# Summing a modulation part's two chunks side by side in a two-block transformer kernel on one Trainium2 core

## What is computed

```
c_act = silu(c)
mod = c_act @ w_mod[l] + b_mod[l]
sh_m, sc_m, g_m, sh_f, sc_f, g_f = split(mod, 6)
h = rms_norm(x, norm_mix_g[l]) * (1.0 + sc_m) + sh_m
x = x + g_m * mixer(h, ...)
h = rms_norm(x, norm_ffn_g[l]) * (1.0 + sc_f) + sh_f
x = x + g_f * moe_ffn(h, ...)
```

## Time and profile before

| | |
|---|---|
| median of 3 runs | 2131.26 us (2130.9 to 2132.2) |
| profiled execution, its own time | 2132.88 us |
| its span, first to last instruction | 2131.1 us |
| PE busy | 2043.1 us (96%) |
| DVE busy | 958.8 us (45%) |
| ACT busy | 404.0 us (19%) |
| mean granted TensorE clock | 0.985 |

### The profile page before, as it was taken

The page is one execution under the profiler, slowest core; times in us unless marked ns, Lnnn a source line. Parts: engine busy times, 40 slices in busy tenths (PEclk is TensorE's granted clock), DMA queues, the critical chain, the costliest instruction groups (busy, mean ns, idle before and its releaser), DMA issues. The chain is left out here.

```text
span 2131.1 us, 29148 instructions
## 1 busy us (share of the span) xinstructions
PE 2043.1 (96%) x10772; PEld 1105.8 (52%) x10772; DVE 958.8 (45%) x1926; ACT 404.0 (19%) x803; POOL 59.6 (3%) x143
## 2 busy tenths in 40 slices
PE   5999999899999999989999989999999997999998
PEld 2845544544545455466544454544545453475475
DVE  3797534433334333359865253333333333253252
ACT  2133211011111111123231111111111111232131
POOL 1000003000000000000000030000000000110000
PEclk9999999999999999999999989999999999999999
DMA  9664548699999999767454448999999997432621
GB/s 348 190 218 173 198 153 339 259 421 405 392 406 401 405 409 391 316 225 229 158 213 182 180 177 334 402 406 399 405 404 400 404 404 249 151 93 68 219 75 45
DMA packets 148386, 599.06 MB, mean 281 GB/s; under 512 B 13052, under 2 KB 17760, under 8 KB 96864
## 3 DMA queue, kind: packets, MB, share of 16 engines
q1 hardware_dynamic: 146912, 595.10, 72.6%
q0 software_dynamic: 1408, 3.10, 0.7%
HBM read 597.11 MB, written 1.05 MB: 281 GB/s over the span
## 5 line engine op out<-in xcount | busy, mean ns | idle before, releaser
L1232 PE MATMUL banks<-weight_ring,h_t 128*64 128x512 f32 x2112 | 464.6, 592 | 3.3 <-DVE h_t L1987 3.3
L867 PE MATMUL banks<-weight_ring,h_t 128*128 128x512 f32 x768 | 335.1, 593 | 2.4 <-issue 1.5
L1232 PEld LDWEIGHTS banks<-weight_ring,h_t 128*64 128x64 f32 x2112 | 152.9, 137 | 302.8 <-issue 301.0
L867 PEld LDWEIGHTS banks<-weight_ring,h_t 128*128 128x128 f32 x768 | 145.1, 190 | 181.2 <-issue 178.7
L1220 PEld LDWEIGHTS banks<-z,sp_ 128*128 128x128 bf16 x3168 | 179.7, 99 | 58.5 <-issue 51.9
L2012 DVE SCALAR_TENSOR_TENSOR o_parts<-banks,slot_weight,o_parts 128x512 fp32r<-128x512 f32 x132 | 99.2, 751 | 245.9 <-ACT o_parts L1523 245.9
L1992 DVE TENSOR_TENSOR z<-banks,z 128x256 f32<-128x256 f32 x66 | 28.1, 425 | 386.4 <-ACT z L1510 386.4
L1220 PE MATMUL banks<-z,sp_ 128*128 128x128 bf16 x3168 | 191.2, 221 | 4.9 <-DVEq L1977 4.9
L1270 PE MATMUL banks<-o_parts,slot_of 128*128 128x512 f32 x528 | 140.7, 408 | 6.0 <-issue 5.6
L1523 ACT ACTIVATE o_parts<-banks,slot_weight 128x512 fp32r<-128x512 f32 x132 | 90.7, 687 | 277.3 <-PE banks L1257 277.3
L2249 PE MATMUL banks<-weight_ring,h_t 128*128 128x512 f32 (+2 forms) x384 | 135.9, 514 | 0.7 <-DMA weight_ring<-in_w_in 0.4
(11 more groups left out here) (479 smaller groups left out, 1896.2 us busy)
## 6 DMA issues: line engine op xcount, KB each, us to landing
weight_ring<-in_w SPq DMA_DIRECT2D x264, 1024.0 KB, 10.0
weight_ring<-in_w_in SPq DMA_DIRECT2D x36, 2048.0 KB, 10.3
slots<-in_w SPq DMA_DIRECT2D x68, 1024.0 KB, 9.2
weight_ring<-in_w_mod SPq DMA_DIRECT2D x24, 2048.0 KB, 11.6
qk<-in_w SPq DMA_DIRECT2D x32, 1024.0 KB, 8.5
z<-in_w SPq DMA_DIRECT2D x32, 1024.0 KB, 10.5
weight_ring<-in_w_out SPq DMA_DIRECT2D x8, 2048.0 KB, 7.8
weight_ring<-in_w_in SPq DMA_DIRECT2D x10, 1024.0 KB, 12.3
```

Source lines behind the costliest of these rows:

```text
L867: mm = nc.tensor.matmul(bank[:, 0:cols], stationary[:, k, t * P:(t + 1) * P], w[:, k, 0:cols], start=(k == 0), stop=(k == KT - 1))
L1232: mm = nc.tensor.matmul(h_bank[own, :], x_blk[:, i, k, own], w13(2 * i + b)[:, :, k, :], start=(k == 0), stop=(k == KT - 1), skip_group_ch ...
```

## The change

Five things are edited.

1. The sum step of the two chunks of a column part becomes one step, `("cols", c)`: chunk `c` is summed with a 64-column stationary into partitions 0 to 63 of a bank, chunk `c + 1` into partitions 64 to 127 of the same bank. VectorE picks once for both, with `ident_half` (the sum of the identity's halves, made once at the start), and `mod_columns` no longer adds halves. Row parts keep their sums.
2. The places: `("sum", 6)` stood after the value projections and is gone; `("cols", 6)` stands ahead of the turns of `a`, `("cols", 8)` behind them; VectorE's pick of chunk 6 moves from behind the rotation to behind `a_ready`, ahead of `mod_on_dve(9)`.
3. `("cols", 12)` stands where the sum of 13 stood, and nothing where the sum of 12 did; `("cols", 14)` replaces two sums.
4. At the start the turns of the tokens stand ahead of the first part; ScalarE takes the norm ahead of its copies; the partial rows go through three buffers instead of two; four banks are skipped.
5. `c` is loaded first, SyncE no longer waits for GpSimd, and TensorE raises the eight bank semaphores in its place.

```diff
 MOD_STEPS = {
-    "start": [("part", 0), ("part", 1), ("sum", 0), ("part", 2), ("sum", 1), ("part", 3), ("sum", 2), ("sum", 3)],
-    "ka": [("sum", 4), ("sum", 5)], "va": [("sum", 6)], "aT": [("sum", 7), ("sum", 8), ("sum", 9)],
+    "first": [("part", 0), ("part", 1), ("cols", 0), ("part", 2), ("pad", 0), ("pad", 1), ("pad", 2), ("pad", 3),
+              ("part", 3), ("cols", 2)],
+    "ka": [("sum", 4), ("sum", 5)], "a": [("cols", 6)], "aT": [("cols", 8)],
     "merged": [("sum", 10), ("sum", 11)],
 }
-MOD_NEXT = {"mT": [("part", 12)], "wo": [("part", 13), ("sum", 12)], "turned": [("part", 14), ("sum", 13)],
-            "rt": [("part", 15), ("sum", 14), ("sum", 15)]}
+MOD_NEXT = {"mT": [("part", 12)], "wo": [("part", 13)], "turned": [("part", 14), ("cols", 12)],
+            "rt": [("part", 15), ("cols", 14)]}
...
-                            pe.wait_ge(B[l]["mod_part", c].free, B[l]["mod_part", c].consumed_at(l))
-                            mm = nc.tensor.matmul(bank[:], K.part_share[:].to_broadcast([P, P]), mod_part[c], start=True, stop=True)
+                            for half in range(2):
+                                own = slice(64 * half, 64 * half + 64)
+                                if c in DVE_CHUNKS:
+                                    pe.wait_ge(dve_parts.sem, dve_parts.at(l, c + half - DVE_CHUNKS[0] + 1))
+                                    share = K.ones[:, 0:64]
+                                else:
+                                    pe.wait_ge(B[l]["mod_part", c + half].free, B[l]["mod_part", c + half].consumed_at(l))
+                                    share = K.part_share[:].to_broadcast([P, 64])
+                                mm = nc.tensor.matmul(bank[own, :], share, mod_part[c + half], start=True, stop=True,
+                                                      skip_group_check=True)
...
-                mod("start")
-
                 norm_turn(0, l)
+                mod("first")
...
-                mod("va")
...
                         branch(2, h, t)
+                mod("a")
                 pe.wait_ge(a_ready.sem, a_ready.at(l))
...
-                mod((6,))
                 conv_taps(28, TAPS)
...
                 dve.drain().then_inc(a_ready.sem, 1)
+                mod(6)
                 mod_on_dve(9)
...
-                mod((7, 8, 9))
+                mod(8)
                 mod_columns(1)
```

More of the change, by code:

```diff
@@ L313, in vector_part @@
         dve.wait_ge(from_pool, masks_ready)
+        nc.vector.tensor_tensor(K.ident_half[:], K.ident[:, 0:64], K.ident[:, 64:P], ALU.add)
+        dve.drain()
         dve.wait_ge(from_act, tables_ready)
@@ L348 @@
 DVE_CHUNKS = range(4, 12)
-MOD_NEXT = {"mT": [("part", 12)], "wo": [("part", 13), ("sum", 12)], "turned": [("part", 14), ("sum", 13)],
-            "rt": [("part", 15), ("sum", 14), ("sum", 15)]}
+MOD_NEXT = {"mT": [("part", 12)], "wo": [("part", 13)], "turned": [("part", 14), ("cols", 12)],
+            "rt": [("part", 15), ("cols", 14)]}
 def mod_steps(place, layer):
-    if place == "start" and layer > 0:
+    if place == "first" and layer > 0:
         return []
@@ L363, in mod_groups @@
 def mod_groups(place, layer):
-    return [("mod_" + what, c) for what, c in mod_steps(place, layer)]
+    return ["-pad" if what == "pad" else ("mod_" + what, c) for what, c in mod_steps(place, layer)]
 def groups_1(layer):
@@ L373, in _groups_1 @@
     return (
-        mod_groups("start", layer) + [("xT", 0, g) for g in range(4)]
+        [("xT", 0, g) for g in range(4)] + mod_groups("first", layer)
         + [(n, i) for n in ("ug", "ua") for i in range(2)] + ["vec"] + [(n, i) for n in ("qc", "kc") for i in range(2)]
@@ L378, in _groups_1 @@
         + [("suf", r, par) for r in range(3) for par in range(2)]
-        + [(n, t) for n in ("vc", "va") for t in range(T)] + mod_groups("va", layer)
+        + [(n, t) for n in ("vc", "va") for t in range(T)]
         + [("oc", i) for i in range(2)]
@@ L383, in _groups_1 @@
         + [x for h in range(2) for t in range(T) for x in branch_groups(2, h, t)]
-        + [("aT1", i) for i in range(2)] + ["aT0"] + mod_groups("aT", layer)
+        + mod_groups("a", layer) + [("aT1", i) for i in range(2)] + ["aT0"] + mod_groups("aT", layer)
         + [("oa", t) for t in range(T)] + [("gt", 0, 0, 0)] + [("oaT", i) for i in range(2)] + [("gt", 0, 0, 1)]
@@ L899, in norm_turn @@
                             mm.then_inc(B[l]["xT", i, g].full, 1)
+            for b in range(BANKS):
+                pe.sem_inc(free[b].sem, 1)
             const_tensor(pe)
@@ L1587, in mod @@
                         else:
-                            v.tensor_tensor(pick, bank[:].rearrange("p (q k) -> p q k", k=KT),
-                                            broadcast(K.ident[:, 64 * half:64 * half + 64], 2, KT), ALU.mult)\
-                                .then_inc(B[l]["mod_sum", c].free, 1)
+                            bank = full_of(("mod_cols", c), l)
+                            v.tensor_tensor(pick, bank[:].rearrange("p (q k) -> p q k", k=KT), broadcast(K.ident_half[:], 2, KT),
+                                            ALU.mult).then_inc(B[l]["mod_cols", c].free, 1)
                             dve.drain()
-                            v.tensor_reduce(col4[:, MOD_COL_PARTS.index(part), half, :], pick.rearrange("p q k -> p k q"),
-                                            AX.X, ALU.add)
+                            v.tensor_reduce(col4[:, MOD_COL_PARTS.index(part), :], pick.rearrange("p q k -> p k q"), AX.X, ALU.add)
                             dve.drain()
@@ L1653, in _ @@
                 if l == 0:
-                    mod(range(MOD_FIRST))
+                    mod(0, 2)
                 if l == 0:
```

37 lines of the change are left out of this document (16 added, 21 removed).

## The result

| | before | changed |
|---|---|---|
| median of 6 runs | 2132.06 us (2130.90 to 2144.93) | 2150.7 us (2147.46 to 2154.06) |
| ratio, 95% interval | | 1.0085 (1.0065 to 1.0105) |
| profiled execution, its own time | 2132.88 us | 2147.46 us |
| its span | 2131.1 us | 2145.7 us |

The changed kernel is slower, as forecast, and by more: 2150.7 where 2144.0 was predicted, 0.7 us beyond the end of the stated range (2150). On the profiled executions the difference is 14.6 us, where the sum said 12.8.

The account below looks back on a forecast made before the run. TensorE, busy 96% of the span, was taken as nearly the critical path. +12.7 + 4.4 − 1.8 − 1.6 − 0.9 = +12.8 us gave 2145.7 us profiled, 2144.0 us against the median; range 2138.5 to 2150.

Parts of the forecast that it names:

- the term of the savings: Sum 6's removal −1.8 us, the start −1.6 and `cols 14` at the router −0.9.
- the way from one profiled execution to a median: Profiled execution forecast at 2145.7 us; its 1.6 us above the median taken off, giving 2144.0.
- The stall: Attention, both layers: TensorE waits for pick and chunk 9's rows; loop 10.25 us for 3.89, +12.7 us in all.
- The off-path rival: Attention: VectorE's loop costs nothing, only savings stay, including −1.7 us at `a`; 2125.3 us, chance 0.03.
- The clock: Behind both attention waits the granted clock falls from 2.4 to 1.2 GHz: 2.2 us per layer, +4.4 us.
- The rivals without the fall: Attention: the wait comes but the clock stays high behind it, −4.4 us, 2139.6 us; chance 0.10.
- with a long one: Attention: small matmuls hold the clock low for longer, +9.2 us over both layers, 2153 us; chance 0.06.
- Sum 6: Chunk 6's sum leaves its old place in two layers, where TensorE had no wait: −1.8 us.
- `cols 14`: Around the router, first layer: one joined step for the two sums of chunks 14 and 15, −0.9 us.
- the start: Kernel start: one pick instead of two, one add less, earlier weights; half clock stays: −1.6 us, ends 0 and −4.
- Halves side by side: Every pair of 64-column halves: the two overlap on TensorE and take 0.86 us a pair.
- Rival "a pass late": At three places on the path a pair's second half begins 0.43 us late: +1.3 us, 2145.3 us; chance 0.15.

Follow-up runs that it names:

- the filled run: Changed kernel with six extra 64-column matmuls per layer in TensorE's wait ahead of the second half of `cols 8`: 2142.11 us, ratio 1.0054.
- The order alone: Kernel before with full sums and its old start and router, only chunk 6's sum and pick moved to the changed places: 2153.88 us, ratio 1.0102.
- a fourth buffer: Changed kernel with a fourth buffer for partial rows, so VectorE makes chunk 9's rows ahead of the pick of chunks 6 and 7: 2133.23 us, ratio 1.0003.
- an earlier sum: Changed kernel with `cols 6` on TensorE between the first branch's two column halves, ahead of VectorE's pick: 2133.93 us, ratio 1.0004.
- the start alone: Kernel before with only the change's edits at the start, all sums from chunk 4 on as before: 2132.12 us, ratio 1.0001.
- The padded kernel before: Kernel before with twelve small dummy matmuls on TensorE at the start, ahead of the first chunk: 2125.30 us, ratio 0.9970.

## Why the prediction was right about the sign and short by 7 us

The step that failed is the term of the savings, −4.3 us, which no median shows; a second one is the way from one profiled execution to a median.

**The stall: right.** Loop without the clock 10.44 us (the filled run) against 10.25 worked out, so +6.55 per layer for +6.35. The order alone makes it, and a fourth buffer or an earlier sum removes it. The idle time was shorter than the 6.4 to 7 us foretold, 5.88, because TensorE's work ahead of it took longer, 3.5 us for 2.6 (a pair takes 1.01 us and not 0.86, and the lone first half of `cols 8` 1.07 and not 0.43); the length of the loop doesn't depend on it. The off-path rival is excluded; and its price, 2125.3 us for a kernel with the savings and no stall, was wrong: two kernels of that kind ran in 2133.2 and 2133.9. Its −1.7 us at `a` did not come either: the loop without the stall is 3.98 us, not 3.89 − 0.86.

**The clock: right.** 2.0 + 2.9 = 4.9 us against 4.4; stall and clock together 2 x 6.55 + 4.9 = 18.0 us by the traces, 16.6 by medians and 18.8 by ratios, against 17.1. The rivals without the fall and with a long one are excluded at these two places.

**The savings, −4.3 us in the sum: this step failed.** Two of its three terms were wrong by mechanism. Sum 6 (−1.8) gave 0.07 us per layer and `cols 14` (−0.9) gave 0.02: both removed sums had covered a wait for ScalarE (0.72 us at L1010, and the copy of part 15). I wrote of sum 6 that TensorE had no wait around it, which was true only because the sum was there. For the sum of chunk 12 I had asked who is late next, and 0.90 us came as said; for 6 and 14 I had not. The third term, the start (−1.6, ends 0 and −4), was larger in this trace, −2.3 us and a shorter low clock (1.4 us lost for 2.9), −3.8 in all. That is near the best of the eleven traces with the new start, whose gains at that place go from 1.3 to 3.9 us with the moment at which the clock falls; the assumption that the fall would stay the same was the weak one. And no median shows any of it: the start alone gives 1.0001, and the fourth-buffer kernel, with all the savings and no stall, 1.0003. Why it is lost further on is open.

**From the profile to the median: it failed too.** The profiled executions agree with the sum rather well: 2 x 6.55 + 4.9 − 0.1 − 3.8 = 14.1 of the 14.6 us between them, where I had 12.8. But I set the changed median 1.6 us below its profiled time, as the kernel before had it. It lay 3.2 us above: the profile had caught the execution with the highest clock, 0.985, where the mean of the twelve was 0.9824. These 4.9 us and the 1.8 make the miss of 6.7. That the two profiled executions came so near the sum is in part luck: the good start of the one stood in for the two savings that failed. By medians the miss reads: 0.8 us because the kernel before itself had 2132.06 in six runs for 2131.26 in three, 4.3 for savings that are not there, and 1.6 for the rest, which is less than the measures of the stall's price differ by.

**Halves side by side: right.** Rival "a pass late", 1.29 us a pair, falls: the passes of both halves start together at 216.00 and 216.48. A pair took 217.01 − 216.00 = 1.01 us where I took 0.86. The Trainium skill ("TensorE: Matmul & The Clock Gate", section "Step-by-step: what each phase is for") says that the matmuls themselves stay in program order. That two halves must follow each other with no overlap, and the 1.29 us, were my reading of it; the trace shows that an order of starts doesn't keep two column halves apart.

**Around the router: right on the 0.90 us**, which did not let the clock fall there, so that rival falls as well. The pair of chunks 12 and 13 brought nothing, as said.

## What to carry to other kernels

When an edit takes work out from between two others, look at what the engine would wait for once it is gone: three of the sums removed here (of chunks 6, 12 and 14) had covered a wait for another engine. An early consumer on an in-order engine costs nothing by its own wait (7.88 us here, harmless), only by what is queued behind it; a buffer more, or the producer moved a few microseconds ahead, takes all of it away. And before sub-microsecond savings are counted, see what the code's position and the clock's scatter do to the kernel: twelve idle dummies brought more, 5 to 6 us, than all savings of this change, and by two ways at once. A kernel with dummies is therefore no neutral witness for the code's position; its trace has to be read at the start too.

## What had not been expected of the hardware

- An idle stretch of 5.56 us on TensorE, with no wait that the profile shows, came and went with dummy instructions ahead of it, at the start or in the first block: present in all eight traces without them, absent in all six with them. The padded kernel before is 0.3% faster, in part by this.
- With twelve small matmuls in a wait at the start, the stretch of low clock that the kernel before has from 30.1 us on lay at 19.3 us, where TensorE waits for weights: 2.36 us gained by the `dw_rows` product. That is one trace with them, against two without (30.1 and, in the order-alone run, 30.4).
- Two 64-column matmuls of float32 into the two halves of a bank, both inputs ready, run both their passes together, within 0.01 us (216.00 and 216.48), 1.01 us the pair; with a wait between them they take 1.79 us, as two whole sums do.
- The mean granted clock of one kernel's executions scatters, and the time with it, 1.6 us per 0.001 over 22 runs of the kernel before: the changed kernel's six runs went from 0.985 (2147.46 us) to 0.980 (2154.06 us).
